# A layer trunk on one Trainium2 core: the delta rule's recurrence and its front, in another order

## The chip, the cores and the metric

The kernel runs on one core of one Trainium2 chip. The metric is the time of one execution on the device, in microseconds (us), and the time of a kernel is the median of several executions.

## The reference: what is computed

The input is 256 frames of width 2048. Two layers are applied, each followed by a squared-ReLU MLP (2048 to 8192 and back), and a last RMSNorm. The first layer mixes in two ways at once: retention (four heads of 256), and RWKV-7 time mixing (sixteen heads of 64), which is where the change lies. The second layer is a gated linear recurrence (RG-LRU), and the change doesn't touch it.

RWKV-7 needs, for each of its sixteen heads, a recurrence over the frames with a state of 64 by 64:

```
sa = S k̂_t ;  S = S diag(w_t) - sa (k̂_t a_t)^T + v_t k_t^T ;  y_t = S r_t
```

The decay w and the rate a ("iclr") come out of two small weights: `decay = exp(-exp(-softplus(-(w0 + tanh(wl) @ w2)) - 0.5))` and `iclr = sigmoid(a0 + al @ a2)`, with `wl` and `al` of 64 columns each. After the recurrence each head is normalised, a bonus is added, and the result is multiplied by a gate.

## The kernel before, in words

**Weight products.** All large weights stream through a ring of four buffers. A group of 512 weight columns has eight units of 256 weight rows. SyncE loads a unit (`load_unit`), ScalarE rounds it into a high part (`split_hi`, L210), VectorE takes the remainder as a low part (`split_lo`, L215), and TensorE multiplies. `multiply_part` (L226 to L228) is one part of a group, three products of 128x128 by 512 columns; a group has 32 parts, four to a unit, and a part whose unit has no low part yet waits for it.

**The delta rule.** `rwkv` runs over eight pairs of heads, p = 0 to 7, one head in the upper 64 partitions and the other in the lower 64. In the same eight blocks TensorE multiplies eight groups of retention's input weights. The order of the two is written out by hand: `more(pe, p, parts, m)` issues the next m parts of block p's group between steps of the delta rule. Block 0 is special, since its first eight parts are issued ahead of the block, and `more` issues only those of its parts that haven't run.

**A block on TensorE** (`rwkv_pe`). First the mean of the block before (`pe_mean`, 128x128). Then products in chunks of 64 frames, four chunks, for two heads each, all 64x64 (`mm_heads`, two instructions, one for each head): the products of the keys (`products_done`) and the transposes (`tokens_done`). Then 3 parts, `pe_variance` of the block before (its variance and its gate's small weights, three 128x128 products of 256 columns), the transpose of the first inverse (`inv_done`), 2 parts, and `pe_front_lora` of the next pair of heads, which is two 128x128 products of 256 columns. They share one loaded weight tile, whose upper 64 rows belong to the decay and lower 64 to the rate. The right operand of each has zeros in the other half.

**The solve.** Five levels follow (l = 1 to 5). Each has a product y, 3 parts, and two products for the inverse and its transpose, which wait for VectorE's `w_inv` (L905) and for ScalarE's and VectorE's copies of the level before.

**The recurrence.** Four chunks, c = 0 to 3. TensorE makes the right side from the state (`rhs_done`), 1 part, waits for ScalarE's copy (`rhs_u`, L999), solves for u (`u_done`), 1 part, waits for ScalarE's copy (`u_neg`, L1001), then adds key times value and beta times u into `tp[0]` (`state_done`) and three products into y. The next chunk waits for VectorE's new state (L942, L944). After the last chunk come the parts that are left.

**A block on VectorE** (`rwkv_dve`). It begins with the centring of the block before, then the masks (L889 to L896), the variance of the block before (L825), a low part, and `dve_front_mix`: the time shift of three 128x256 tiles of the next pair of heads, in six instructions of differences (L638, L639) and three of L698. Only then comes level 1's `w_inv`. At the end of a block stand the next group's low parts 0 and 1. Part 1 waits for ScalarE's high part 1, which comes behind the copy of the whole group's result.

**The others.** ScalarE (`rwkv_act`) reads the small weights' products in `act_front_tanh`, both out of `acc[1]`. GpSimd (`rwkv_pool`) masks five levels, from block 4 on rotates retention's queries and keys, and loads the small weights of later blocks with DMAs, after `variance_done` and `lora_done`. Each engine's program is in order, and the engines meet only by semaphores.

Of the kernel before, what the change touches and what calls it, by code (L numbers as in the profile page):

```python
# [6 lines left out]
ACT = mybir.ActivationFunctionType  # L7
# [4 lines left out]
P = 128  # L12
T = 256
# [41 lines left out]
def trunk(nc, x_in, params, consts, cossin, rdecay, ev_w_in, ev_w_out, rw_w2, rw_a2, rw_g2, od_w_in, gx_w, ga_w,  # L55
          od_w_out, ff_w1, ff_w2, final_norm, out):
    ctx = ExitStack()
    with ctx:
# [690 lines left out]

        def act_front_tanh(act, q, bank=acc[1]):  # L750

            act.wait_ge(sem("lora_done"), q + 1)
            act.activation(thw_t, bank[:, 0:T], ACT.Tanh, scale=0.5,
                           bias=half_bias[:, 0, bass.ds(q, 1)]).then_inc(sem("tanh_ready"), 1)
            act.activation(iclr_t, bank[:, T:2 * T], ACT.Tanh, scale=0.5,
                           bias=half_bias[:, 1, bass.ds(q, 1)]).then_inc(sem("tanh_ready"), 1)
# [24 lines left out]
        ones = con[:, CONES:CONES + P]  # L781
        eye = con[:, CEYE:CEYE + CHUNK]

        def pe_front_lora(pe, q, bank=acc[1]):
# [29 lines left out]
        def dve_centre(dve, n, bank=acc[0]):  # L814

            dve.wait_ge(sem("mean_done"), n + 1)
            dve.scalar_tensor_tensor(cen_t, bank[:, 0:T], -1.0 / CHUNK, out_t, ALU.mult, ALU.add).then_inc(sem("centred"), 1)
# [59 lines left out]
        def rwkv_dve(dve, p, norm, front):  # L877
# [3 lines left out]
            front_own = Own(dve, "front_own", q, 7)  # L881
            norm_own = Own(dve, "norm_own", p - 1, 4)
            if norm:
                dve_centre(dve, p - 1)
                dve.wait_ge(sem("state_ready"), 3 * p)
# [14 lines left out]
            split_lo(dve, g, 2)  # L900
            if front:
                dve_front_mix(dve, q)
            for l in range(1, LEVELS):
# [56 lines left out]
            else:  # L960
                split_lo(dve, g + 1, 0)
            split_lo(dve, g + 1, 1)
            own.end()
# [63 lines left out]
        def rwkv_pe(pe, p, norm, front, parts):  # L1027
# [19 lines left out]
            pe.wait_ge(stg_written, 2 * (RET_STG + p))  # L1047
            more(pe, p, parts, 3)
            if norm:
                pe_variance(pe, p - 1)  # L1050
            pe.wait_ge(sem("inv_start"), p + 1)
# [3 lines left out]
            last.then_inc(sem("inv_done"), 1)  # L1055
            more(pe, p, parts, 2)
            if front:
                pe_front_lora(pe, p + 1)
            pe.wait_ge(sem("seen_ready"), p + 1)
# [23 lines left out]
            for c in range(NCHUNK):  # L1083
                s, v = state[:, c % 2, :], v_tok[:, c, :]
                if c:
                    pe.wait_ge(sem("state_ready"), 3 * p + c)
                    mm_heads(tp[2][:, 0:CHUNK], kappa_in[:, c, :], s, last=False)
                mm_heads(tp[2][:, 0:CHUNK], seen_v[:, c, :], v, first=(c == 0)).then_inc(sem("rhs_done"), 1)
                more(pe, p, parts, 1)
                if c == 0:  # L1090
                    if front:
                        pe.wait_ge(sem("kk_sum_read"), p + 2)
                    else:
                        pe.wait_ge(sem("gated"), p)
                    mm(acc[0][:, 0:T], ones, sq_t).then_inc(sem("bonus_done"), 1)
                    pe.wait_ge(sem("inv_ready"), LEVELS * (p + 1))
                pe.wait_ge(sem("rhs_ready"), NCHUNK * p + c + 1)
                mm_heads(tp[3][:, 0:CHUNK], inv_t[:, c, :], rhs_u[:, :]).then_inc(sem("u_done"), 1)
                more(pe, p, parts, 1)
                pe.wait_ge(sem("u_ready"), NCHUNK * p + c + 1)  # L1100
                if c < NCHUNK - 1:
                    mm_heads(tp[0][:, 0:CHUNK], key_tok[:, c, :], v, last=False)
                    mm_heads(tp[0][:, 0:CHUNK], beta_tok[:, c, :], u_neg[:, :], first=False).then_inc(sem("state_done"), 1)
                y = chunks(tp[1][:, 0:T])[:, c, :]
                if c:
                    mm_heads(y, s, rho_in[:, c, :], last=False)
                mm_heads(y, v, seen_y_key[:, c, :], first=(c == 0), last=False)
                last = mm_heads(y, u_neg[:, :], seen_y_beta[:, c, :], first=False)
            last.then_inc(sem("out_done"), 1)
            more(pe, p, parts, 32)  # L1110

        def first_front(role, eng, j):
# [15 lines left out]
            elif role == "act":  # L1128
                if j == 3:
                    rwkv_prepare_act(eng)  # L1130
                if j == 6:
                    act_front_square(eng, 0)
                    act_front_v(eng, 0)
                if j == 7:
                    split_hi(eng, RET_N, 0)
                    act_front_tanh(eng, 0, acc[3])
                    act_front_exp(eng, 0)
                    act_front_root(eng, 0)
            elif role == "pe":
                if j == 6:  # L1140
                    once(eng, "masks_landed", 16)
                    once(eng, "lora_inputs", 4)
                    eng.wait_ge(stg_written, 12)
                    pe_front_sum(eng, 0, acc[2])
                    pe_front_lora(eng, 0, acc[3])
# [714 lines left out]
```

## Time and profile before

| | |
|---|---|
| time before, median of 3 runs | 2434.14 us (2434.02 to 2436.7) |
| the profiled execution's own time | 2431.89 us |
| its span in the trace | 2430.2 us |
| mean granted TensorE clock | 0.991 of full |
| TensorE busy | 2362.7 us, 97% |
| VectorE busy | 1475.5 us, 61% |
| ScalarE busy | 1098.6 us, 45% |
| the eight blocks of the delta rule | about 180 to 563 us of the span |

Times in a timeline are microseconds from the span's start. A row gives start, duration, engine, line, operation, the tile written and the tiles read, and the count; in brackets is how long the engine sat idle ahead of it and whom it waited for. PE is TensorE, DVE is VectorE, ACT is ScalarE, POOL is GpSimd. An f32 product shows as two records, so a line "x16" is eight instructions. A record is longer than the distance to the next one, because products overlap in the array; distances between starts are what the work takes.

### The profile page before, as it was taken

What the parts mean: (1) busy time and instruction counts of PE and PEld (TensorE: products, weight loads), DVE (VectorE), ACT (ScalarE), POOL (GpSimd) and SP (SyncE); (2) the same over time, 40 slices, a digit from 0 to 9 for tenths busy, and PEclk for the clock granted to TensorE, in tenths of its full rate; (3) what the DMA queues carried; (4) which work ended last, traced back from release to release, by engine and by line L of the source; (5) the groups of instructions that cost most, each with busy time, mean ns of one, the idle gap of its engine ahead of it and who ended that gap; (6) DMA issues with size and microseconds to landing.
All of it is one profiled execution on the core that took longest, in us unless ns stands there. A gap on an engine that the chain in (4) does not pass through costs nothing.

```text
span 2430.2 us, 36910 instructions
## 1 busy us (share of the span) xinstructions
PE 2362.7 (97%) x14214; PEld 1976.4 (81%) x14214; DVE 1475.5 (61%) x1645; ACT 1098.6 (45%) x1405; POOL 237.5 (10%) x184
## 2 busy tenths in 40 slices
PE   7999999999999999999999999989999999999997
PEld 7877777777888888888888888878888888888886
DVE  5456666765566466566566566775665565565664
ACT  5444444434544344344344445754543343343443
POOL 0002113421000000000000001220000000000001
PEclk9999999999999999999999999999999999999999
DMA  7653333333556666666666665556566566566654
GB/s 220 185 153 91 91 95 90 91 99 113 184 177 200 193 185 191 196 184 190 193 189 190 188 202 165 163 167 190 183 191 193 166 190 196 165 189 193 190 190 157
DMA packets 215464, 411.67 MB, mean 169 GB/s; under 512 B 13264, under 2 KB 19792, under 8 KB 215184
## 3 DMA queue, kind: packets, MB, share of 16 engines
q1 hardware_dynamic: 213888, 406.94, 54.5%
q0 software_dynamic: 1424, 2.49, 0.4%
q8 instruction: 121, 1.98, 0.3%
q14 instruction: 31, 0.25, 0.0%
HBM read 407.28 MB, written 2.10 MB: 168 GB/s over the span
## 4 chain that ended last, share of the span: by engine, by line
PE 92%; DVE 3%; issue 2%; ACT 2%; POOL 0%; DMA 0%; DVEq 0%; SPq 0%; ACTq 0%
PE acc_pair L226 19%; PE acc_pair L227 18%; PE acc_pair L228 18%; PE acc_pair L242 10%; PE tp_pair L242 10%; PE tp_pair L244 5%; PE acc_pair L244 5%; PE tp_pair L773 5%; PE acc_pair L773 1%; PE tp_pair L367 1%; DVE stg L724 1%; PE acc_pair L1569 1%; PE tp_pair L1569 1%; DVE w_lo L215 0%; ACT L766 0%
## 5 line engine op out<-in xcount | busy, mean ns | idle before, releaser
L215 DVE TENSOR_TENSOR w_lo<-raw,w_hi 128x1024 fp32r<-128x1024 f32 (+1 forms) x760 | 1014.8, 1339 | 764.3 <-ACT w_hi L210 758.0
L210 ACT ACTIVATE w_hi<-raw 128x1024 fp32r<-128x1024 f32 (+1 forms) x760 | 800.9, 1055 | 919.4 <-PE acc_pair L228 578.9
L242 PE MATMUL acc_pair<-xT_both,w_hi 128*128 128x512 f32 x1024 | 322.8, 397 | 12.1 <-issue 12.1
L242 PE MATMUL tp_pair<-xT_both,w_hi 128*128 128x512 f32 x1024 | 319.4, 393 | 0.0
L226 PE MATMUL acc_pair<-w_hi,xT_both 128*128 128x512 f32 (+1 forms) x736 | 301.9, 410 | 4.3 <-DVE w_lo L215 4.3
L227 PE MATMUL acc_pair<-w_lo,xT_both 128*128 128x512 f32 (+1 forms) x736 | 286.2, 389 | 0.0
L228 PE MATMUL acc_pair<-w_hi,xT_both 128*128 128x512 f32 (+1 forms) x736 | 285.9, 388 | 0.0
L226 PE MATMUL acc_pair<-w_hi,hidA_hi 128*128 128x512 f32 x640 | 251.9, 394 | 6.3 <-DVE hidA_lo L1603 6.3
L226 PE MATMUL acc_pair<-w_hi,hidB_hi 128*128 128x512 f32 x640 | 251.0, 392 | 0.0
L227 PE MATMUL acc_pair<-w_lo,hidA_hi 128*128 128x512 f32 x640 | 250.8, 392 | 0.0
L228 PE MATMUL acc_pair<-w_hi,hidA_lo 128*128 128x512 f32 x640 | 250.4, 391 | 0.0
L228 PE MATMUL acc_pair<-w_hi,hidB_lo 128*128 128x512 f32 x640 | 249.5, 390 | 0.0
L227 PE MATMUL acc_pair<-w_lo,hidB_hi 128*128 128x512 f32 x640 | 249.4, 390 | 0.0
L242 PEld LDWEIGHTS tp_pair<-xT_both,w_hi 128*128 128x128 f32 x1024 | 193.5, 189 | 44.0
L339 POOL TENSOR_TENSOR stg<-stg,rstd_row 128x1024 f32<-128x1024 f32 x32 | 76.7, 2396 | 1350.1 <-DVE stg L422 1350.1
L244 PE MATMUL tp_pair<-xT_both,w_lo 128*128 128x256 f32 x1024 | 207.5, 285 | 0.0
L242 PEld LDWEIGHTS acc_pair<-xT_both,w_hi 128*128 128x128 f32 x1024 | 177.9, 191 | 35.4 <-issue 12.9
L244 PE MATMUL acc_pair<-xT_both,w_lo 128*128 128x256 f32 x1024 | 205.7, 283 | 0.0
L244 PEld LDWEIGHTS acc_pair<-xT_both,w_lo 128*128 128x128 f32 x1024 | 177.2, 191 | 20.1
L226 PEld LDWEIGHTS acc_pair<-w_hi,xT_both 128*128 128x128 f32 x736 | 139.4, 189 | 36.0 <-DVE xT_both L432 3.8
L228 PEld LDWEIGHTS acc_pair<-w_hi,xT_both 128*128 128x128 f32 x736 | 139.4, 189 | 28.6
L244 PEld LDWEIGHTS tp_pair<-xT_both,w_lo 128*128 128x128 f32 x1024 | 159.8, 192 | 0.0
(237 smaller groups left out, 2400.3 us busy)
## 6 DMA issues: line engine op xcount, KB each, us to landing
raw<-in_ff_w SPq DMA_DIRECT2D x512, 512.0 KB, 4.3
raw<-in_ev_w_in SPq DMA_DIRECT2D x112, 512.0 KB, 3.6
raw<-in_od_w_in SPq DMA_DIRECT2D x64, 512.0 KB, 4.2
raw<-in_ev_w_out SPq DMA_DIRECT2D x32, 512.0 KB, 3.6
raw<-in_od_w_out SPq DMA_DIRECT2D x32, 512.0 KB, 4.3
raw<-in_ev_w_in SPq DMA_DIRECT2D x8, 288.0 KB, 5.3
x<-in_x_in SPq DMA_DIRECT2D x4, 512.0 KB, 6.0
gate_w<-in_gx_w SPq DMA_DIRECT2D x8, 256.0 KB, 2.8
```

Source lines behind the costliest of these rows:

```text
L210: act.activation(w_hi[:, j % RING, :, 0:wide], raw[:, j % RING, :, 0:wide], ACT.Copy).then_inc(hi_ready, 1)
L215: dve.tensor_tensor(w_lo[:, j % RING, :, 0:wide], raw[:, j % RING, :, 0:wide], w_hi[:, j % RING, :, 0:wide], ALU.subtract).then_inc(lo_rea ...
L226: nc.tensor.matmul(o, hi[:, tok], wh, start=(kt == 0), stop=False)
L227: nc.tensor.matmul(o, hi[:, tok], wl, start=False, stop=False)
L228: last = nc.tensor.matmul(o, lo[:, tok], wh, start=False, stop=(kt == KT - 1))
L242: nc.tensor.matmul(o[:, :], w_hi[:, j % RING, kt % KU, c * P:(c + 1) * P], both, start=(kt == 0), stop=False)
L244: last = nc.tensor.matmul(o[:, T:2 * T], w_lo[:, j % RING, kt % KU, c * P:(c + 1) * P], xT_both[:, kt, 0, :], start=False, stop=(kt == KT ...
L339: pool.tensor_tensor(by_tile(hid_sum), by_tile(hid_sum), row, ALU.mult).then_inc(scaled_ready, 1)
L367: last = nc.tensor.transpose(tp[2 * b + c // 2][0:s.shape[1], (c % 2) * T + h * P:(c % 2) * T + (h + 1) * P], s, ident)
L724: own(dve.reciprocal(nrm_t, nrm_t))
L773: return nc.tensor.matmul(out, lhsT, rhs, start=first, stop=last)
L1569: last = nc.tensor.matmul(odd_gate_banks(v, n)[i][:, jh * T:(jh + 1) * T], gate_w[:, n % 2, i, ih, jh * P:(jh + 1) * P], conv[:, 2 * n + i ...
```

## The change

On VectorE, `dve_front_mix` moves from behind the block's low part 2 to the very start of the block, and the low part of unit 1 moves from the end of a block to behind that mix in the next block (in the last block both low parts stay at the end). On TensorE, the 3 and 2 parts around the inverse's transpose become 5 parts ahead of it; `pe_variance` moves behind that transpose; `pe_front_lora` becomes `pe_front_lora_heads` in blocks 0 to 6: four products of 64x64 weight quarters by 256 columns, two for the decay into `acc[1]`, two for the rate into `tp[3]`, out of which ScalarE now reads the rate. In the recurrence, the products into y that need the state and the values, and the product of keys and values, move ahead of the solve for u; the part behind the right side stays only in chunk 0, and the part behind u becomes two. A block has 29 parts ahead of its last product then, and 3 behind it, where it had 28 and 4.

```diff
--- before.py
+++ after.py
@@ -747,12 +747,12 @@
             act.wait_ge(sem("mixed"), 3 * q + 3)
             act.activation(b_t, z_at(q, K_BLOCK), ACT.Square, scale=pcol_at("k_k", q)).then_inc(sem("kk_square"), 1)
 
-        def act_front_tanh(act, q, bank=acc[1]):
+        def act_front_tanh(act, q, bank=acc[1], rate=tp[3][:, 0:T]):
 
             act.wait_ge(sem("lora_done"), q + 1)
             act.activation(thw_t, bank[:, 0:T], ACT.Tanh, scale=0.5,
                            bias=half_bias[:, 0, bass.ds(q, 1)]).then_inc(sem("tanh_ready"), 1)
-            act.activation(iclr_t, bank[:, T:2 * T], ACT.Tanh, scale=0.5,
+            act.activation(iclr_t, rate, ACT.Tanh, scale=0.5,
                            bias=half_bias[:, 1, bass.ds(q, 1)]).then_inc(sem("tanh_ready"), 1)
 
         def act_front_exp(act, q):
@@ -780,6 +780,15 @@
 
         ones = con[:, CONES:CONES + P]
         eye = con[:, CEYE:CEYE + CHUNK]
+
+        def pe_front_lora_heads(pe, q):
+
+            pe.wait_ge(sem("front_lora_landed"), 32 * (q + 1))
+            pe.wait_ge(sem("tanh_ready"), 2 * q)
+            for m in (slice(0, CHUNK), slice(CHUNK, P)):
+                mm(acc[1][m, 0:T], lora_w[0:CHUNK, 0, m], lora_in[0:CHUNK, 0, :])
+                last = mm(tp[3][m, 0:T], lora_w[CHUNK:P, 0, m], lora_in[CHUNK:P, 1, :])
+            last.then_inc(sem("lora_done"), 1)
 
         def pe_front_lora(pe, q, bank=acc[1]):
 
@@ -880,7 +889,10 @@
             own = Own(dve, "dve_own", p, 4)
             front_own = Own(dve, "front_own", q, 7)
             norm_own = Own(dve, "norm_own", p - 1, 4)
+            if front:
+                dve_front_mix(dve, q)
             if norm:
+                split_lo(dve, g, 1)
                 dve_centre(dve, p - 1)
                 dve.wait_ge(sem("state_ready"), 3 * p)
             own(dve.tensor_copy(decay_end[:, :], decay[:, :, CHUNK]))
@@ -898,8 +910,6 @@
             if norm:
                 dve_variance(dve, p - 1)
             split_lo(dve, g, 2)
-            if front:
-                dve_front_mix(dve, q)
             for l in range(1, LEVELS):
                 dve.wait_ge(sem("y_done"), 5 * p + l)
                 dve.tensor_tensor(w_inv[:, :, :], over_chunks(CEYE, CHUNK), chunks(tp[2][:, 0:T]), ALU.subtract)\
@@ -959,7 +969,7 @@
                 dve_front_rho(dve, q)
             else:
                 split_lo(dve, g + 1, 0)
-            split_lo(dve, g + 1, 1)
+                split_lo(dve, g + 1, 1)
             own.end()
 
         def rwkv_act(act, p, norm, front):
@@ -1045,17 +1055,16 @@
                     last = mm_heads(chunks(tp[1][:, i * T:(i + 1) * T])[:, c, :], t[:, c, :], eye)
             last.then_inc(sem("tokens_done"), 1)
             pe.wait_ge(stg_written, 2 * (RET_STG + p))
-            more(pe, p, parts, 3)
-            if norm:
-                pe_variance(pe, p - 1)
+            more(pe, p, parts, 5)
             pe.wait_ge(sem("inv_start"), p + 1)
             pe.wait_ge(sem("tokens_ready"), 2 * p + 2)
             for c in range(NCHUNK):
                 last = mm_heads(chunks(tp[1][:, 0:T])[:, c, :], inv_t[:, c, :], eye)
             last.then_inc(sem("inv_done"), 1)
-            more(pe, p, parts, 2)
+            if norm:
+                pe_variance(pe, p - 1)
             if front:
-                pe_front_lora(pe, p + 1)
+                pe_front_lora_heads(pe, p + 1)
             pe.wait_ge(sem("seen_ready"), p + 1)
             for l in range(1, LEVELS):
                 pe.wait_ge(sem("level_ready"), 5 * p + l)
@@ -1082,29 +1091,30 @@
                     last.then_inc(sem("inv_t_done"), 1)
             for c in range(NCHUNK):
                 s, v = state[:, c % 2, :], v_tok[:, c, :]
+                y = chunks(tp[1][:, 0:T])[:, c, :]
                 if c:
                     pe.wait_ge(sem("state_ready"), 3 * p + c)
                     mm_heads(tp[2][:, 0:CHUNK], kappa_in[:, c, :], s, last=False)
                 mm_heads(tp[2][:, 0:CHUNK], seen_v[:, c, :], v, first=(c == 0)).then_inc(sem("rhs_done"), 1)
-                more(pe, p, parts, 1)
                 if c == 0:
+                    more(pe, p, parts, 1)
                     if front:
                         pe.wait_ge(sem("kk_sum_read"), p + 2)
                     else:
                         pe.wait_ge(sem("gated"), p)
                     mm(acc[0][:, 0:T], ones, sq_t).then_inc(sem("bonus_done"), 1)
                     pe.wait_ge(sem("inv_ready"), LEVELS * (p + 1))
-                pe.wait_ge(sem("rhs_ready"), NCHUNK * p + c + 1)
-                mm_heads(tp[3][:, 0:CHUNK], inv_t[:, c, :], rhs_u[:, :]).then_inc(sem("u_done"), 1)
-                more(pe, p, parts, 1)
-                pe.wait_ge(sem("u_ready"), NCHUNK * p + c + 1)
-                if c < NCHUNK - 1:
-                    mm_heads(tp[0][:, 0:CHUNK], key_tok[:, c, :], v, last=False)
-                    mm_heads(tp[0][:, 0:CHUNK], beta_tok[:, c, :], u_neg[:, :], first=False).then_inc(sem("state_done"), 1)
-                y = chunks(tp[1][:, 0:T])[:, c, :]
                 if c:
                     mm_heads(y, s, rho_in[:, c, :], last=False)
                 mm_heads(y, v, seen_y_key[:, c, :], first=(c == 0), last=False)
+                if c < NCHUNK - 1:
+                    mm_heads(tp[0][:, 0:CHUNK], key_tok[:, c, :], v, last=False)
+                pe.wait_ge(sem("rhs_ready"), NCHUNK * p + c + 1)
+                mm_heads(tp[3][:, 0:CHUNK], inv_t[:, c, :], rhs_u[:, :]).then_inc(sem("u_done"), 1)
+                more(pe, p, parts, 2)
+                pe.wait_ge(sem("u_ready"), NCHUNK * p + c + 1)
+                if c < NCHUNK - 1:
+                    mm_heads(tp[0][:, 0:CHUNK], beta_tok[:, c, :], u_neg[:, :], first=False).then_inc(sem("state_done"), 1)
                 last = mm_heads(y, u_neg[:, :], seen_y_beta[:, c, :], first=False)
             last.then_inc(sem("out_done"), 1)
             more(pe, p, parts, 32)
@@ -1133,7 +1143,7 @@
                     act_front_v(eng, 0)
                 if j == 7:
                     split_hi(eng, RET_N, 0)
-                    act_front_tanh(eng, 0, acc[3])
+                    act_front_tanh(eng, 0, acc[3], acc[3][:, T:2 * T])
                     act_front_exp(eng, 0)
                     act_front_root(eng, 0)
             elif role == "pe":
```

## Rows read from the trace of the kernel before

**Rows 1.** The page's busy times: busy us, share of the span, instructions.

```profile
PE 2362.7 (97%) x14214; PEld 1976.4 (81%) x14214; DVE 1475.5 (61%) x1645; ACT 1098.6 (45%) x1405; POOL 237.5 (10%) x184
```

**Rows 2.** Waits of TensorE, 175 to 560 us: total us, times, longest.

```profile
PE tp_pair L773 <- DVE w_inv L905: 7.9, 4, 3.0
PE tp_pair L773 <- DVE state L944: 2.4, 7, 0.4
...
PE tp_pair L773 <- ACT tokens L972: 0.8, 1, 0.8
```

**Rows 3.** Timeline of TensorE in block 5, from the variance to level 1.

```profile
421.59 0.59 PE L773 MATMUL acc_pair<-stg,con 128*128 128x256 f32 x2
...
422.98 0.68 PE L773 MATMUL tp_pair<-con,inv_t 64*64 64x64 f32 x16
...
425.10 1.02 PE L773 MATMUL acc_pair<-lora_in,lora_w 128*128 128x256 f32 x4
426.05 0.68 PE L773 MATMUL tp_pair<-inv,level_a 64*64 64x64 f32 x16
426.67 0.50 PE L226 MATMUL acc_pair<-w_hi,xT_both 128*128 128x512 f32 x1
...
428.61 0.39 PE L228 MATMUL acc_pair<-w_hi,xT_both 128*128 128x512 f32 x1
430.61 0.68 PE L773 MATMUL tp_pair<-w_inv,inv_t 64*64 64x64 f32 x16 [1.61 <-DVE w_inv L905]
```

**Rows 4.** Timeline of VectorE in block 5, and the start of block 6.

```profile
423.08 0.42 DVE L825 TENSOR_SCALAR stg<-acc_pair 128x256 f32<-128x256 f32 x1 [0.54 <-PE acc_pair L773]
423.43 1.55 DVE L215 TENSOR_TENSOR w_lo<-raw,w_hi 128x1024 fp32r<-128x1024 f32 x1
424.90 0.95 DVE L638 TENSOR_TENSOR stg<-z 128x255 f32 x1
...
430.15 0.41 DVE L905 TENSOR_TENSOR w_inv<-con,tp_pair 128x256 f32<-128x256 f32 x1
...
467.03 1.23 DVE L215 TENSOR_TENSOR w_lo<-raw,w_hi 128x1024 fp32r<-128x1024 f32 x1 [4.86 <-ACT w_hi L210]
```

**Rows 5.** Timeline of VectorE, two rows of the mix in block 1.

```profile
235.23 0.41 DVE L638 TENSOR_TENSOR stg<-z 128x255 f32 x1
...
236.02 1.26 DVE L698 SCALAR_TENSOR_TENSOR z<-stg,par,z 128x256 f32 x3
```

**Rows 6.** Timeline of TensorE in block 0: level 1's inverse.

```profile
190.26 0.88 PE L773 MATMUL tp_pair<-w_inv,inv_t 64*64 64x64 f32 x16 [3.04 <-DVE w_inv L905]
```

**Rows 7.** Stretches: us, then busy us and records of PE, PEld, DVE, ACT, POOL; clock; DMA.

```profile
190.60:194.00 3.40, 3.40 (x47) 3.09 (x44) 2.27 (x4) 2.80 (x4) 0.00 (x0) 0.50 0.43 101
225.00:272.80 47.80, 46.71 (x548) 35.38 (x547) 31.31 (x59) 20.44 (x40) 6.96 (x9) 1.00 0.32 92
```

**Rows 8.** Timeline of VectorE in block 0: the first mask.

```profile
181.92 0.69 DVE L889 TENSOR_TENSOR by_beta<-tp_pair,con 128x512 f32<-128x512 f32 x1 [1.26 <-PE tp_pair L773]
```

**Rows 9.** Timeline of TensorE in block 5: the recurrence's chunks 1 and 2.

```profile
453.10 0.33 PE L773 MATMUL tp_pair<-rhs_u,inv_t 64*64 64x64 f32 x4
...
454.43 0.28 PE L773 MATMUL tp_pair<-u_neg,tokens 64*64 64x64 f32 x4
454.54 0.28 PE L773 MATMUL tp_pair<-seen,state 64*64 64x64 f32 x4
...
455.10 0.33 PE L773 MATMUL tp_pair<-state,seen 64*64 64x64 f32 x4
...
456.37 0.33 PE L773 MATMUL tp_pair<-rhs_u,inv_t 64*64 64x64 f32 x4
```

**Rows 10.** Timeline of ScalarE in block 5: the right side's copy of chunk 2.

```profile
455.59 0.22 ACT L999 ACTIVATE rhs_u<-tp_pair 128x64 f32<-128x64 f32 x1 [1.59 <-PE tp_pair L773]
```

**Rows 11.** Timeline of VectorE in block 5: the states of chunks 2 and 3.

```profile
454.76 0.28 DVE L944 SCALAR_TENSOR_TENSOR state<-tp_pair,decay_end,scaled 128x64 f32<-128x64 f32 x1 [1.53 <-PE tp_pair L773]
...
458.36 0.28 DVE L944 SCALAR_TENSOR_TENSOR state<-tp_pair,decay_end,scaled 128x64 f32<-128x64 f32 x1
```

## The prediction

> **What bounds the kernel now.** First the busy times: TensorE works for 97% of the span [rows 1], so time is saved only where TensorE waits, or where its own work gets shorter. Next its waits while the eight blocks of the delta rule run. One is large: 7.9 us for `w_inv`, in four places, the longest 3.0 us [rows 2]. The other three are then (7.9 - 3.0) / 3 = 1.6 us each. The states of the recurrence cost 2.4 us in seven waits, and the tokens 0.8 once [rows 2].
>
> The timelines show where they lie. In block 5 TensorE's last product before level 1's inverse starts at 428.61; with 0.23 for it and 0.09 for the change to 64-row products the inverse could start at 428.94. It starts at 430.61, 1.67 us late [rows 3]. VectorE explains it: its low part ends, the mix starts at 424.90, and `w_inv` can only start behind it at 430.15, 5.25 us later [rows 4]. That mix is slow there, since GpSimd works beside it: the first difference takes 0.95 where one in block 1 takes 0.41 [rows 4, 5]. At the start of the next block the same engine waits 4.86 us for ScalarE's high part 1 [rows 4]. In block 0 the wait for `w_inv` is 3.04 us [rows 6], and the granted clock is 0.50 (1.2 GHz) from 190.6 to 194.0, just behind that idle time; elsewhere in such blocks it is 1.00 (2.4 GHz) [rows 7]. So the waits for the mix are the only large ones, in blocks 4, 5, 6 and 0.
>
> **The mix moves on VectorE.** In a quiet stretch it costs three differences of 0.41, three short ones, and 1.26 for the last three, 2.4 to 2.7 us [rows 5]. It moves into a gap of 4.86 us [rows 4], in which GpSimd's work has not begun (it waits for the mask that comes later). So the mix ends some 2.2 us before ScalarE's high part is there, and I cost it at nothing from block 1 on. Were the gap gone, centring, masks and the inverse's start would slip by up to 2.7 us a block, but five parts stand ahead of the inverse now (below). The low part of unit 1 changes its place in the program, not its time: it waits for the same high part, and nothing stands between. No DMA is issued in these steps on SyncE; its loads wait for low parts whose times stay.
>
> At the old place, what is late next? The variance now comes behind the inverse's transpose. VectorE's read of it waits for that, and behind this read, in VectorE's queue, stand low part 2 and `w_inv`. TensorE ends the variance at about 425.1 in block 5 (next paragraph); 0.35 for the read and 1.55 for the low part [rows 4] give 427.0, so `w_inv` is there at 427.5. TensorE wants it at about 428.9. The cover is 1.4 us and the wait goes whole: 3 x 1.67 = 5.0 us. GpSimd's loads wait for the variance and for the small weights' products as well, yet are needed a block later; they stand behind its masks and rotations anyway.
>
> In block 0 the gap is shorter: VectorE waits only 1.26 us before its first mask [rows 8]. The mix delays the masks by 2.4 - 1.26 = 1.1 us or a little more. TensorE has idle time of 0.8 for the tokens there [rows 2], and five parts that have run already cover nothing. I charge 0.3 us (between 0 and 1.4; nearer 0, as the transpose of the inverse already starts late). Against it, the mix is gone from the path to `w_inv`; of the wait of 3.04 [rows 6] some 0.5 stays for the mask and low part that remain there, charge included: -2.6 us. With no such idle time the clock should stay up. TensorE is busy for all 3.40 us at 0.50 [rows 7]; half of that, 1.7, is what full clock could give back at most, and 0 if the clock falls all the same. The waits for copies between the products don't halve, so I take a little less than the upper bound, to which the busy row is nearer: another -1.2 us. Block 0: -3.8 us.
>
> **The parts and the variance on TensorE.** Three parts take 1.94 + 0.23 = 2.17 us [rows 3]: 0.69 each (three products at 0.23) and 0.10 more for the first one behind 64-row products. Before, in block 5: 3 parts 2.18, variance and gate 422.98 - 421.59 = 1.39, the transpose (0.61, as y) and two parts 425.10 - 422.98 = 2.12, the front's two products 0.95, y 0.62 [rows 3], in all 7.26. After: 5 parts 3.56, 0.09 for the change, the transpose 0.61, variance 1.39 (0.10 for its first, less the 0.09 that moves), 0.14 for the next change and a first weight load, the new front L, y 0.56. That is 6.35 + L.
>
> **The front in quarters.** A record of 256 columns takes 0.214 us by the distances (0.95 = four, and 0.09 for the change) [rows 3]. Four quarters are eight records. The trace before has no two quarters of the same rows or columns in flight together; the nearest rows are the head pairs, in opposite quarters: y's eight instructions (16 records of 64 columns) take 0.62, changes included [rows 3], so such a pair takes as long as one instruction alone. By that, L is 2 x 0.43 = 0.86. Bounds: one after the other 1.71; all four at once 0.43. I take 0.86, since pairs are what the trace shows. The block's front is then 7.21, 0.05 less, which I count as nothing. ScalarE reads the rate out of `tp[3]`, whose masks were read before and which the recurrence writes long after: nothing.
>
> The Trainium skill, in TensorEngine Tiling (Array Packing), section Tiling Modes, says that in 64x64 mode the array is four independent tiles that load and multiply in parallel. No row here shows more than two. By it L would be 0.43.
>
> **The recurrence.** From the right side's first product to ScalarE's start, copy and wake-up is about 0.78 us (455.59 - 455.10 = 0.49, 0.22, and 0.06 as between a state's end at 455.04 and TensorE's start at 455.10) [rows 9 to 11]; the two pairs of the right side and three pairs moved there fill some 0.63, at 0.11 a pair and a longer first one [rows 9]. So TensorE now waits 0.14, where a part covered it and the solve came 1.27 behind the start [rows 9]. From the solve, two parts and two changes take 1.83. From the beta product, VectorE starts after 0.33 and takes 0.28 [rows 9, 11]; with the wake-up and a longer first pair the next chunk starts at 0.72, and only one pair of y lies beside it, not three: 0.4 us of new idle time. A turn is 0.78 + 1.83 + 0.72 = 3.33, before 3.27 (453.10 to 456.37) [rows 9]. The one after it is VectorE's: its two states lie 3.60 apart, the second starting without a wait for TensorE [rows 11], held by its own work between them, in both orders. So a turn costs +0.06 or nothing. Chunk 0 has two more pairs ahead of its solve, +0.23, and two fewer stand behind the last one, -0.28. Three changes fewer of 0.19 are in these sums. A block: 0. Bounds: all new idle time laid on top, 3 x (0.4 + 0.14) = +1.6; or hidden, with three changes saved, -0.6. I take 0, as a sum of rows, not of bounds. Eight blocks: -5 to +12.7.
>
> **The sum.** -5.0 - 3.8 = -8.8 us. The profiled execution took 2431.89 (its span 2430.2), 2.25 below the median of 2434.14, so it would be 2423.1, and the median 2425.3.
>
> **Rivals.**
> *The four quarters run at once.* Seven blocks save 0.43 more each, 3.0 us: 2422.3. For it: head pairs do overlap fully. Against: no row has two products that share rows.
> *They run one after the other.* Seven times +0.86: +6.0, 2431.3.
> *The recurrence's copies show.* Half of the upper bound, 0.8 us a block, +6.4: 2431.7. For it: the cover of both copies shrinks, and TensorE already waits for the state up to 0.4 us [rows 2]. Against: the reckoning above, in which the work between two states sets the longest turn.
> *The wait for `w_inv` stays in blocks 4 to 6*, because the variance holds VectorE up instead of the mix. Only block 0 gains: 2430.3. Against: 1.4 us of cover.
> *The clock falls in the recurrence: slower.* Many small waits with 64x64 products between them, and the clock granted goes from 2.4 to 1.2 GHz as it did in block 0. 3.4 us at half cost 1.7 [rows 7]. Once in each block is +13.6 (2438.9), twice 2452.5; from eight such falls on the kernel is slower. Against: the clock is 1.00 through block 1 with its waits [rows 7], and new waits are under 0.5 us, the one ahead of the fall was 3.04.
> The Trainium skill, in TensorE: Matmul & The Clock Gate, Part 1, says that a quiet array is throttled to half its rate. Block 0's row agrees; no row shows it for such short gaps.
>
> **How the numbers follow.** About 0.2%, 4.9 us, can be told from no change: faster is below 2429.3, slower above 2439.0. Forecast 0.48 (2425.3), four at once 0.27, one after the other 0.06, copies 0.09, `w_inv` 0.06, clock 0.04. Faster: the first two, and 0.05 of the others where they come out half: 0.80. Slower 0.04, same 0.16. The range takes in the first two with runs 2 us off, and `w_inv`: 2419.5 to 2430.5.
>
> **What would show it.** Right: `w_inv` is no longer among TensorE's waits but for about 0.5 us in block 0; no clock of 0.50 near 190; VectorE's mix takes 2.4 us just behind `rho` with the low part at its old time; blocks 1 to 3 keep their length and blocks 4 to 6 get 1.7 us shorter; y starts 0.9 us behind the quarters' first record. Wrong: y 0.5 behind it (four at once) or 1.8 (in a row); waits of over 0.5 us ahead of the solves or states; or a new wait for `w_inv`, with VectorE reading the variance late.

## The result, and the profile after

The changed kernel takes 2409.6 us (median; 2407.56 to 2410.24), the kernel before 2434.65 beside it: a ratio of 0.9895, 95% interval 0.9882 to 0.9907. That is 25 us less, where the prediction had 8.8 and a range down to 2419.5.

The page's busy times, to be held against [rows 1]:

```profile
PE 2348.9 (98%) x14242; PEld 1967.9 (82%) x14242; DVE 1467.2 (61%) x1645; ACT 1100.1 (46%) x1405; POOL 235.6 (10%) x184
```

TensorE is 98% busy in a shorter span (2405.8 us, the execution's own time 2407.56). TensorE's waits in the eight blocks, 175 to 560 us (total us, times, longest), against [rows 2]:

```profile
PE tp_pair L773 <- DVE state L954: 6.1, 16, 0.5
PE tp_pair L773 <- DVE state L952: 2.2, 8, 0.3
...
PE tp_pair L773 <- DVE inv_t L905: 1.2, 1, 1.2
...
PE tp_pair L773 <- DVE w_inv L915: 0.5, 1, 0.5
```

The wait for `w_inv` is down from 7.9 us in four places to 0.5 in one. The states cost more: 8.3 us in sum (6.1 and 2.2), where they cost 3.6 before. The next fence is TensorE's timeline in block 5, from its first product to block 6's; it answers to [rows 3].

```profile
408.80 1.09 PE L773 MATMUL tp_pair<-seen,beta_in 64*64 64x128 f32 x16
...
415.71 0.68 PE L773 MATMUL tp_pair<-con,inv_t 64*64 64x64 f32 x16
...
416.86 1.38 PE L773 MATMUL acc_pair<-lora_in,lora_w 128*128 128x256 f32 x5
417.82 0.43 PE L773 MATMUL tp_pair<-lora_in,lora_w 64*64 64x256 f32 x1
417.83 0.43 PE L773 MATMUL acc_pair<-lora_in,lora_w 64*64 64x256 f32 x1
417.84 0.43 PE L773 MATMUL tp_pair<-lora_in,lora_w 64*64 64x256 f32 x1
418.08 0.38 PE L773 MATMUL acc_pair<-lora_in,lora_w 64*64 64x256 f32 x1
...
418.11 0.38 PE L773 MATMUL tp_pair<-lora_in,lora_w 64*64 64x256 f32 x1
418.30 0.64 PE L773 MATMUL tp_pair<-inv,level_a 64*64 64x64 f32 x16
...
421.17 0.68 PE L773 MATMUL tp_pair<-w_inv,inv_t 64*64 64x64 f32 x16
...
455.67 1.09 PE L773 MATMUL tp_pair<-seen,beta_in 64*64 64x128 f32 x16
```

Three things are to be seen. The inverse of level 1 (421.17) has no bracket any more. The front's quarters (L773, 64*64, 64x256; the first of the eight records hides in the "x5" row, and two of the second four are left out) start in two clumps of four, at 417.8 and 418.1, and y starts at 418.30, 0.49 us behind the first of them. And a block is 455.67 - 408.80 = 46.87 us long. VectorE in the same block and at the start of the next, against [rows 4, 5]:

```profile
417.93 0.42 DVE L834 TENSOR_SCALAR stg<-acc_pair 128x256 f32<-128x256 f32 x1 [2.70 <-PE acc_pair L773]
...
419.67 0.41 DVE L915 TENSOR_TENSOR w_inv<-con,tp_pair 128x256 f32<-128x256 f32 x1
...
453.89 0.42 DVE L638 TENSOR_TENSOR stg<-z 128x255 f32 x1 [0.40 <-DVE seen L742]
...
455.09 1.27 DVE L698 SCALAR_TENSOR_TENSOR z<-stg,par,z 128x256 f32 x3
457.68 1.23 DVE L215 TENSOR_TENSOR w_lo<-raw,w_hi 128x1024 fp32r<-128x1024 f32 x1 [1.32 <-ACT w_hi L210]
```

The variance is read at 417.93, `w_inv` is done at 420.08, and TensorE wants it at 421.17. The mix runs from 453.89 in a quiet stretch and ends 1.3 us ahead of the low part, which stands where it stood. In block 0:

```profile
184.62 0.59 PE L773 MATMUL tp_pair<-con,inv_t 64*64 64x64 f32 x13 [1.22 <-DVE inv_t L905]
...
187.06 0.68 PE L773 MATMUL tp_pair<-w_inv,inv_t 64*64 64x64 f32 x16 [0.51 <-DVE w_inv L915]
```

3.04 us of waiting [rows 6] have become 0.51, and 0.78 for the tokens 1.22. The clock stays at 1.00 there.

**Where the 24.4 us of the two spans went.** The starts of the blocks' first products, and of the last products before the jumps, give the table.

| stretch | before | after | difference |
|---|---|---|---|
| to block 0's first product | 180.72 | 180.04 | -0.7 |
| block 0 | 44.89 | 41.31 | -3.6 |
| blocks 1 to 3, each | 47.2 | 46.87 | -0.33 |
| blocks 4 to 6, each | 48.9 | 46.87 | -2.0 |
| the second MLP, from its loop's first jump back to the second | 183.95 | 177.45 | -6.5 |
| from the second jump back to the end of the span | 328.57 | 321.86 | -6.7 |

From block 0's first product to block 7's the delta rule gave -10.7 us (333.2 to 322.5). From there to the second MLP's first jump the two kernels differ by 0.3 us. More than half of the 24.4 us lies in a stage that the change doesn't touch. The second MLP's loop runs three times on TensorE and jumps back twice. Its timeline before, around the first jump:

```profile
1917.54 0.40 PE L244 MATMUL tp_pair<-xT_both,w_lo 128*128 128x256 f32 x2
1922.91 1.22 PE L242 MATMUL acc_pair<-xT_both,w_hi 128*128 128x512 f32 x2 [4.97 <-issue]
```

And after:

```profile
1906.42 0.40 PE L244 MATMUL tp_pair<-xT_both,w_lo 128*128 128x256 f32 x2
1907.59 0.72 PE L242 MATMUL acc_pair<-xT_both,w_hi 128*128 128x512 f32 x2 [0.78 <-issue]
```

"issue" is time in which TensorE waited for nothing that the profile shows. Over the whole kernel, L242's idle time for issue was 12.1 us in four places, the longest 5.1, and is now 3.7, the longest 1.3; the four places are the jumps of both MLPs. The granted clock behind the first long jump of the kernel before (columns as in [rows 7]):

```profile
1922.90:1928.00 5.10, 5.09 (x16) 4.32 (x17) 0.49 (x1) 0.00 (x0) 0.00 (x0) 0.50 0.37 106
```

So 5.25 and 5.36 us from product to product instead of 1.05 (4.2 and 4.3 more), and some 5 us of products at half clock behind each (2.3 and 2.4 more): 6.5 and 6.7 us for the two jumps, 13.2 in all.

### The profile page after: what moved, and what is told of

Same layout as the page of the kernel before. It is cut to its first block, busy times and chain, and to the rows that moved or that the text cites. A ratio compares the mean times of both kernels' runs of the same rounds, so it can differ in the third digit from the quotient of the medians.

```text
span 2405.8 us, 36946 instructions
## 1 busy us (share of the span) xinstructions
PE 2348.9 (98%) x14242; PEld 1967.9 (82%) x14242; DVE 1467.2 (61%) x1645; ACT 1100.1 (46%) x1405; POOL 235.6 (10%) x184
## 4 chain that ended last, share of the span: by engine, by line
PE 93%; DVE 3%; ACT 2%; issue 1%; POOL 0%; DMA 0%; SPq 0%; DVEq 0%; ACTq 0%
PE acc_pair L226 19%; PE acc_pair L227 18%; PE acc_pair L228 18%; PE acc_pair L242 10%; PE tp_pair L242 10%; PE tp_pair L244 5%; PE acc_pair L244 5%; PE tp_pair L773 5%; PE acc_pair L773 1%; PE tp_pair L367 1%; DVE stg L724 1%; PE acc_pair L1579 1%; PE tp_pair L1579 1%; ACT L766 0%; DVE w_lo L215 0%
## 5 line engine op out<-in xcount | busy, mean ns | idle before, releaser
L242 PE MATMUL acc_pair<-xT_both,w_hi 128*128 128x512 f32 x1024 | 320.7, 394 | 3.7 <-issue 3.7
L242 PE MATMUL tp_pair<-xT_both,w_hi 128*128 128x512 f32 x1024 | 317.2, 391 | 0.0
L242 PEld LDWEIGHTS tp_pair<-xT_both,w_hi 128*128 128x128 f32 x1024 | 192.3, 188 | 43.8
L244 PE MATMUL tp_pair<-xT_both,w_lo 128*128 128x256 f32 x1024 | 206.3, 283 | 0.0
L244 PE MATMUL acc_pair<-xT_both,w_lo 128*128 128x256 f32 x1024 | 204.5, 281 | 0.0
L242 PEld LDWEIGHTS acc_pair<-xT_both,w_hi 128*128 128x128 f32 x1024 | 176.5, 190 | 26.9 <-issue 4.5
L244 PEld LDWEIGHTS acc_pair<-xT_both,w_lo 128*128 128x128 f32 x1024 | 176.0, 190 | 20.0
L244 PEld LDWEIGHTS tp_pair<-xT_both,w_lo 128*128 128x128 f32 x1024 | 158.9, 191 | 0.0
```

Source lines behind the costliest of these rows:

```text
L242: nc.tensor.matmul(o[:, :], w_hi[:, j % RING, kt % KU, c * P:(c + 1) * P], both, start=(kt == 0), stop=False)
L244: last = nc.tensor.matmul(o[:, T:2 * T], w_lo[:, j % RING, kt % KU, c * P:(c + 1) * P], xT_both[:, kt, 0, :], start=False, stop=(kt == KT ...
```

## The experiments

All are kernels of this case with one edit. The loops of both MLPs have 1876 instructions on TensorE. Where they start in the compiled program can be told as so many instructions behind a multiple of 256. These counts are mine, from the compiled program; no view of the profile shows them. The four quarters make TensorE's code longer by 56 instructions and the new recurrence makes it 8 shorter, so the places moved by 48: from 76 and 232 (first, second MLP) to 124 and 24.

**Only the place of the code.** In `e1_before_shift`, the kernel before gets this at the start of TensorE's program. The 96 waits are 48 instructions in the compiled program, on a semaphore that was reached long before:

```diff
+            for _ in range(96):
+                pe.wait_ge(sem("rw_zeroed"), 7)
             pe.wait_ge(tables_landed, 32)
```

> The kernel before, with 96 more waits at the start of TensorE's program, on a semaphore that was reached long before (48 instructions in the compiled program, run while TensorE waits for the first data). Nothing else changes, but all of TensorE's code lies 48 instructions later, as in the changed kernel: the loop of the second MLP starts 24 instructions behind a multiple of 256, where it started 232 behind one. Theory A (more than half of the change's gain has nothing to do with the delta rule: the jump back of that loop costs about 5 us where its 1876 instructions touch nine blocks of 256, and about 1.3 us, without a fall of the clock, where they touch eight): idle time of L242 on TensorE falls from 12.1 to about 4 us, no clock of 0.5 near 1921 and 2105 us, the eight blocks of the delta rule as before (46.9 to 48.9 us each), and the time falls by 12 to 14 us, to about 2421. Rival B (the later stages are faster because the data or the loads stand otherwise after the new order of the delta rule): no change, 2434.

2421.33 us (2419.11 to 2423.42), ratio 0.9946 (0.9930 to 0.9963), 13.1 us less than the kernel before beside it. Its waits:

```profile
PE tp_pair L773 <- DVE w_inv L905: 7.9, 4, 3.0
...
PE acc_pair L242 <- issue: 3.7, 4, 1.1
```

`w_inv` is what it was, the jumps are cheap, and the clock is no longer at 0.5 near 1921 and 2105 us. A kernel with the delta rule untouched is 13 us faster by where its code lies. (In the profiled execution block 5 was 1.5 us longer than its sisters, behind a fall of the clock at 432 us; that counts against it.)

**Only VectorE's part.** `e2_mix_only`:

```diff
+            if front:
+                dve_front_mix(dve, q)
             if norm:
+                split_lo(dve, g, 1)
                 dve_centre(dve, p - 1)
...
             split_lo(dve, g, 2)
-            if front:
-                dve_front_mix(dve, q)
...
                 split_lo(dve, g + 1, 0)
-            split_lo(dve, g + 1, 1)
+                split_lo(dve, g + 1, 1)
```

> The kernel before with only VectorE's part of the change: the mix of the next pair of heads at the start of a block, and the low part of unit 1 behind it. TensorE's program and its place are those of before. My reckoning: the waits for w_inv in blocks 4, 5, 6 (1.6 us each) and most of that in block 0 (3.0) go, and the fall of the clock at 190 us with it: -8 to -9 us, 2425.5; the two long jumps of about 5 us at 1918 and 2102 us stay. Rival: without the variance behind the transpose, nothing differs for VectorE, so all of it shows here as well; if the new order of variance and parts is what frees w_inv, the waits stay at over 1 us and the gain is under 4 us.

2424.22 us (2421.94 to 2425.68), ratio 0.9955 (0.9939 to 0.9972), 10.2 us less.

```profile
PE acc_pair L242 <- issue: 11.7, 4, 5.3
...
PE tp_pair L773 <- DVE w_inv L906: 0.5, 1, 0.5
```

Block 0 takes 41.20 us, all others 47.2. The mix gives nearly all of the delta rule's gain, and the long jumps stay. The predicted -8.8 us for this part is right: 3.7 in block 0 and 1.7 in each of blocks 4 to 6 by the trace. (The medians' 10.2 has an interval of 6.8 to 14.9, so it can't say more than that.)

**The front whole again.** `e3_front_whole`, from the changed kernel, with 48 instructions ahead that keep the loops in cheap places:

```diff
-                pe_front_lora_heads(pe, p + 1)
+                pe_front_lora(pe, p + 1)
...
-def act_front_tanh(act, q, bank=acc[1], rate=tp[3][:, 0:T]):
+def act_front_tanh(act, q, bank=acc[1], rate=acc[1][:, T:2 * T]):
```

> The changed kernel with the front's small weights in two whole 128x128 products again, both into acc[1], in place of four quarters; 48 instructions of waits at the start of TensorE's program hold the MLPs' loops in the place where jumps are cheap (116 and 16 behind a multiple of 256). Theory: the four quarters run at once and take 0.47 us where two whole products take 0.95; the whole form also adds one change between 128-row and 64-row products. So blocks 1 to 6 get 0.4 to 0.6 us longer than 46.87, and the time goes up by 3 to 4 us over the changed kernel, to about 2413. Rival (the quarters give nothing, and the 0.33 us by which blocks 1 to 3 got shorter come from the recurrence): no change.

2411.29 us (2410.24 to 2413.8). The blocks are 47.3 us, 0.44 longer, and block 0 0.5 longer: 3.1 us in seven blocks by the trace, as expected. The medians lie only 1.7 us apart, less than the 3 to 4 expected (2.9 against the changed kernel's later median of 2408.44, below); their ranges touch, so the length of the blocks is the evidence here and not the total. The gate's four records and the front's four, then y:

```profile
418.57 1.89 PE L773 MATMUL acc_pair<-lora_in,lora_w 128*128 128x256 f32 x8
420.39 0.68 PE L773 MATMUL tp_pair<-inv,level_a 64*64 64x64 f32 x16
```

Eight records in 1.82 us: the front's two whole products take half of that, 0.91, where the quarters took 0.49. The quarters do run at once.

**The recurrence in its old order.** `e4_old_recurrence` puts the old loop over chunks back into the changed kernel:

```diff
+                more(pe, p, parts, 1)
                 if c == 0:
-                    more(pe, p, parts, 1)
...
+                more(pe, p, parts, 1)
+                pe.wait_ge(sem("u_ready"), NCHUNK * p + c + 1)
+                if c < NCHUNK - 1:
+                    mm_heads(tp[0][:, 0:CHUNK], key_tok[:, c, :], v, last=False)
...
-                more(pe, p, parts, 2)
```

> The changed kernel with the recurrence in its old order: one part behind the right side and one behind u in each chunk, products into y and key times value behind the solve. The loops lie 132 and 32 behind a multiple of 256, where jumps are cheap. My reckoning gave the recurrence's new order nothing (between -0.6 and +1.6 us a block). From the two traces, block 1 to 6 are 0.33 us shorter and the quarters give 0.48, so the new recurrence rather costs 0.1 us a block: the old one would give blocks of 46.8 us and a time within 1 us of the changed kernel's 2409.6. Rival (the new order saves the three changes of product size in each block, 0.19 each): blocks 0.4 to 0.6 us longer, time 3 to 5 us up.

2406.64 us (2405.89 to 2407.64), 3.0 below the changed kernel's 2409.6, where it was expected within 1; blocks of 46.79 us, 0.08 shorter than the changed kernel's, as expected. The changed kernel and this one once more, on one chip:

> The changed kernel as it is, beside the others of this call on the same chip. 2409.6 us by its runs so far.

> The changed kernel with the recurrence in its old order once more, beside the changed kernel itself in this call. The blocks of the first run were 46.79 us against 46.87, 0.6 us in eight blocks; so 0.5 to 3 us less than the changed kernel here. Rival: the 3 us between the two medians of separate calls were the chip's, and the two agree within 0.5 us.

2408.44 (2407.72 to 2409.18) and 2406.22 us (2405.41 to 2406.92): the old order is 2.2 us faster, with ranges that don't touch. But the profiled executions of the two lie 2.6 us apart, and of these only 0.5 are the blocks; 1.7 lie ahead of block 0 (180.44 and 178.71), where the two programs are the same. That the recurrence is worth more than 0.5 us is not shown. The timeline of the changed kernel shows the turn's cost, from chunk 0's last products to chunk 2's solve in block 5:

```profile
442.31 0.33 PE L773 MATMUL tp_pair<-u_neg,tokens 64*64 64x64 f32 x4
...
443.03 0.33 PE L773 MATMUL tp_pair<-state,seen 64*64 64x64 f32 x4 [0.27 <-DVE state L952]
...
443.90 0.33 PE L773 MATMUL tp_pair<-rhs_u,inv_t 64*64 64x64 f32 x4
...
445.75 0.33 PE L773 MATMUL tp_pair<-u_neg,tokens 64*64 64x64 f32 x4
...
447.25 0.33 PE L773 MATMUL tp_pair<-rhs_u,inv_t 64*64 64x64 f32 x4
```

The solve (443.90) comes 0.87 behind the chunk's start (443.03), not 1.27 as in [rows 9]; but the state's wait is 0.27 where it was 0.15, since one pair of products stands beside VectorE's work and not three. From solve to solve it is 3.35 us (443.90 to 447.25; 3.33 reckoned) against 3.27 before: gain and loss nearly cancel, as reckoned.

**Which place is dear?** A jump is called dear here when it costs clearly more than the 0.9 to 2.0 us that the others take. Theory A said: a loop is dear that touches nine blocks of 256 instructions. `e5_shift60` moves the changed kernel's code by 60 more, in the same way as above.

> The changed kernel with 60 more instructions at the start of TensorE's program, run while it waits for the first data. The loop of the first MLP then starts 184 behind a multiple of 256 and touches nine blocks of 256 instructions (184 + 1876 = 2060, over 2048); the loop of the second starts 84 behind one and touches eight. Theory A (it is the number of blocks that the loop touches): now the first MLP's two jumps back, near 887 and 1065 us, cost about 5 us each and the clock falls behind them, the second's stay at about 1.2, and the time is 12 to 14 us above the changed kernel's: 2422. Rival C (a jump is dear only when its target has few instructions left in its block of 256: 24 in the kernel before): with 72 left, enough for some 4 us of work, the jump stays cheap and the time stays at 2410.

2410.69 us (2408.91 to 2413.38), and no jump over 1.66 us from product to product. (It is 2.3 us above the changed kernel on the same chip. A longer row of waits is not free: TensorE's first product starts at 9.7 us here, 11.4 with 76 instructions, 13.5 with 96, and at 5.9 in the changed kernel; block 0 starts 3.3, 4.1 and 4.5 us later.) Theory A falls in this form. Its rival (dear is a target with few instructions left in its block) left open how few are few, and where a block begins; it is theory D from here on. And A could still hold with another boundary. Four more places follow, each run once, so their times are single values; what counts is the jumps in their traces:

> The changed kernel with 76 more instructions at the start of TensorE's program: the first MLP's loop starts 200 behind a multiple of 256, 56 instructions ahead of the next one, the second's 100 behind one. Theory D (a jump fetches the block of its target, which takes 1.1 us, and the next block arrives only some 4 us later; it is dear when the target's block has too few products left to cover that): 56 instructions hold some 25 products at 0.23 us, 5.8 us of work, so all four jumps stay at 1.0 to 1.7 us. Theory A (nine blocks touched, with the blocks' boundary 12 to 16 instructions off): 5.3 us at both jumps near 890 and 1068.

2415.49 us. Around the first MLP's first jump:

```profile
890.85 0.40 PE L244 MATMUL tp_pair<-xT_both,w_lo 128*128 128x256 f32 x2
892.19 0.72 PE L242 MATMUL acc_pair<-xT_both,w_hi 128*128 128x512 f32 x2 [0.94 <-issue]
892.75 0.63 PE L242 MATMUL tp_pair<-xT_both,w_hi 128*128 128x512 f32 x2
893.22 0.62 PE L242 MATMUL acc_pair<-xT_both,w_hi 128*128 128x512 f32 x2
893.68 0.62 PE L242 MATMUL tp_pair<-xT_both,w_hi 128*128 128x512 f32 x2
894.14 0.40 PE L244 MATMUL acc_pair<-xT_both,w_lo 128*128 128x256 f32 x2
894.37 0.40 PE L244 MATMUL tp_pair<-xT_both,w_lo 128*128 128x256 f32 x2
894.61 0.40 PE L244 MATMUL acc_pair<-xT_both,w_lo 128*128 128x256 f32 x2
894.85 0.28 PE L244 MATMUL tp_pair<-xT_both,w_lo 128*128 128x256 f32 x1
896.59 0.38 PE L244 MATMUL tp_pair<-xT_both,w_lo 128*128 128x256 f32 x1 [1.46 <-issue]
```

The jump costs 0.94 us of idle time, then 15 products run (8 of L242, 7 of L244), then TensorE is idle for 1.46. My expectation was wrong there, since it put the boundary at the multiple of 256. The loop starts at 200 with five instructions that are no products, and a product is two instructions: the fetched code ends at 200 + 5 + 30 = 235.

> The changed kernel with 96 more instructions at the start: the first MLP's loop starts 220 behind a multiple of 256, the second's 120. Theory D with the earlier boundary: 13 to 17 instructions, some five products of 0.23 us, lie in the fetched block, so a jump shows 1.1 us, about 1 us of products, and a second idle time of 2 to 3 us. Theory D with the boundary at the multiple: 36 left, 15 products, 3.5 us of work, a second idle time under 0.7. Theory A: 5.3 us in one piece.

2421.96 us.

```profile
890.00 0.40 PE L244 MATMUL tp_pair<-xT_both,w_lo 128*128 128x256 f32 x2
891.78 0.72 PE L242 MATMUL acc_pair<-xT_both,w_hi 128*128 128x512 f32 x2 [1.38 <-DVE stg L422]
892.34 0.62 PE L242 MATMUL tp_pair<-xT_both,w_hi 128*128 128x512 f32 x2
892.80 0.39 PE L242 MATMUL acc_pair<-xT_both,w_hi 128*128 128x512 f32 x1
895.54 0.80 PE L242 MATMUL acc_pair<-xT_both,w_hi 128*128 128x512 f32 x1 [2.35 <-issue]
```

Five products, then 2.35 us of idle time, as the earlier boundary has it: 220 + 5 + 10 = 235 again. The clock falls to 0.50 in this idle time, at 893.7 us, and again at the loop's second jump, at 1078.0. The two jumps cost 5.0 and 4.8 us more than the changed kernel's, and the later start another 4.4. And at 232 only the leading instructions are ahead of 235, no product at all, which is the one long idle time of the kernel before.

> The kernel before with 12 more instructions at the start of TensorE's program: the second MLP's loop starts 244 behind a multiple of 256, where it started at 232. Theory A, and theory D with blocks that begin at a multiple of 256: still dear, 4 to 5.4 us at both jumps near 1918 and 2102. Theory D with a boundary 19 to 23 instructions earlier, so that at 232 only the loop's five leading instructions lay in the fetched block: cheap now, 1.0 to 1.7 us.

> The kernel before with 28 more instructions at the start: the second MLP's loop starts 4 behind a multiple of 256. Theory A with its shifted boundary: dear, 5.3 us at 1918 and 2102. Theory D: cheap, 1.0 to 1.7 us, and the time about 2421.

2420.98 and 2419.02 us. With the second MLP's loop at 244 and at 4, its jumps take 1.06 to 1.48 us, and the clock doesn't fall there. Theory A with its boundary moved would have them dear at 4, theory D with a boundary at 256 at 244. Theory D with the boundary at 235 holds at every place tried:

| start of a loop, behind a multiple of 256 | products in the fetched code | jump, product to product |
|---|---|---|
| 232 | 0 | 5.3 to 5.5 us in one piece |
| 220 | 5 | 1.7 to 2.0, then 2.3 to 2.7 |
| 200 | 15 | 1.2 to 1.9, then 0.9 to 1.7 |
| 184 | 23 | 1.2 to 1.7 |
| 244, 4, 24, 76, 124 and others | 49 and more | 1.7 at most |

The trace's fetches of code fit. At each of the 52 jumps of the thirteen kernels with loops, dear or cheap, one fetch of 16 KB starts 1.1 to 1.9 us ahead of the start of the last product, and the next 2.4 to 3.6 us behind it, 0.9 to 1.0 us long. The queue of the kernel before in 1914 to 1924 us, around its first dear jump, has just these two, at 1915.9 and 1920.7:

```profile
q8 instruction: 2, 0.03, 1.5%
```

The second has landed at 1921.7 and the dear loop goes on at 1922.91. In all eight dear jumps (places 232, 220 and 200) the long wait ends 5.25 to 5.62 us behind the last product, however many products ran before. That is why 23 products are enough: about 1.2 us and 23 times 0.23 are 6.5 us, more than the wait for the next code (an estimate from these rows). That the wait and the fetch are cause and effect is inferred from their times.

The Trainium skill, in Runtime: NRT & Kernel Launch, section Instruction fetch mechanics, says that code comes in 16 KiB blocks of 256 instructions, fetched in sequence ahead of use, and that a taken branch breaks this. The page of the kernel before, in its list of queues (packets, MB, share of 16 engines), agrees in the size, 16.4 KB a packet:

```profile
q8 instruction: 121, 1.98, 0.3%
```

It agrees in the branch as well, by the table above. That the block behind the target's is what hurts, it doesn't say.

**No jumps at all.** `e8_unrolled` has the old recurrence in the changed kernel, and TensorE's MLPs written out:

```diff
-            with eng.Fori(0, QUARTERS - 1) as q:
+            def quarter(q):
...
+            if role == "pe":
+                for q in range(QUARTERS - 1):
+                    quarter(q)
+            else:
+                with eng.Fori(0, QUARTERS - 1) as q:
+                    quarter(q)
```

> As the one with the recurrence in its old order, and TensorE's program of both MLPs written out without a loop (three quarters one behind the other, the other engines keep their loops); the work is the same. Theory A (a jump back waits for code, straight code doesn't, since its next block is fetched ahead): the four idle times of L242 for issue, 3.2 us in sum, and the rest of each jump's 1.3 us between two products go: -4 to -5.5 us, to about 2402. Rival: straight code over 28 thousand instructions is fetched too late as well, and the waits move elsewhere: no change or slower.

2401.94 us (2401.14 to 2403.31), 4.3 less than `e7_old_rec_again` on the same chip; ratio to the kernel before 0.9876 (0.9860 to 0.9893). No idle time for issue is left at L242. This version beats both kernels.

## Why the prediction was wrong, and where it was right

- *The mix.* Right. -5.0 us in blocks 4 to 6 and -3.8 in block 0 were forecast; the mix alone gave three times 1.7 and 3.7. The cover of 1.4 us for `w_inv` behind the later variance was 1.1, and the mix ended 1.3 us ahead of the low part where 2.2 were forecast.
- *Block 0.* The first mask came 1.3 us later (1.1 forecast) and the wait ahead of the inverse grew by 0.4 us (0.3 charged). The clock didn't fall.
- *The parts and the variance.* Right: the inverse's transpose starts 3.62 us behind the first part (412.09 to 415.71; 3.65 reckoned).
- *The front in quarters.* Wrong term: L was put at 0.86 by the head pairs, and measured 0.49. The rival "at once" (0.43, chance 0.27) held, and with it the rule of the Trainium skill's page TensorEngine Tiling (Array Packing), section Tiling Modes. It is worth 3 us in seven blocks.
- *The recurrence.* Right in size: 0 was forecast, +0.08 us a block measured. The three changes of product size saved are given back to the state's trip.
- *The sum.* This is the step that failed: "-5.0 - 3.8 = -8.8 us" takes the rest of the program as fixed. For the delta rule it nearly holds: -8.8, the quarters' -3.1 and the recurrence's +0.6 make -11.3, and -10.7 was measured; the rest is in block 0. But the 48 instructions that the edit adds to TensorE's program moved the second MLP's loop from 232 to 24, and gave 13.2 us by the traces (13.1 by `e1_before_shift`), more than all that the change was about. The kernel before had that loop at the dearest of the places tried; its page showed it, as 12.1 us of idle time for "issue" at L242, and its trace a clock of 0.50 behind. The prediction called the waits for the mix "the only large ones", which is true of 175 to 560 us, the stretch whose waits it went by, and put the rest at nothing without a reason.
- *Slower.* The clock did not fall in the recurrences of the changed kernel.

## What to carry to other kernels

The time that the profile showed as "issue" ahead of a loop's first product, at every turn, went with the place of the code behind the jump, and adding or taking away instructions anywhere ahead of the loop can change it. So a change's own gain is only read in its own stage, block by block, and a comparison of totals needs a control that shifts the code alone. Here, writing out two loops of three turns each was worth another 4.3 us over the cheap places, and makes the place of the loop a question no more.

## What the runs showed of the hardware

- After a jump back, TensorE's next product came 0.9 to 2.0 us behind the last one (0.23 within the loop) wherever the target's block still held a product. The products behind that block came no sooner than 5.25 to 5.62 us behind it; where the block ran out before, the engine stood idle until then (up to 1.46 us with 15 products, 2.35 with five, 4.97 to 5.26 with none).
- Such an idle time took the clock with it: to 0.50 (1.2 GHz) at the 5 us of the kernel before, which made a gap that was 4.2 us longer cost 6.5, and at the 2.35 us of `e12_shift96`. At the 1.46 us of `e9_shift76` it stayed at 1.00.
- Four 64x64 products in the four quarters of the array run side by side: eight records of 256 columns take 0.49 us, where two whole f32 products take about 0.9. Here the two quarters of the same rows write to one bank, the two row halves to different banks.
- The boundaries of the fetched code lay some 21 instructions ahead of the multiples of 256 in the compiled program, as worked out from the products counted at 200 and 220. Why they lie there stays open.
